# Row remainders of 64, a halved w3 product and a later weight split in the expert stage of a hybrid decoder layer

## The chip, the cores and the metric

The kernel runs on one core of a Trainium2 chip. The metric is the device time of one execution in microseconds (us), lower is better. The engines are named as in the profile: PE (TensorE matmul) and PEld (its weight loads), DVE (VectorE), ACT (ScalarE), POOL (GpSimd), SP (SyncE, here only the issuer of DMAs). PSUM is the memory that PE writes its products to.

## The reference, cut to what matters

One decoder layer over 2048 tokens of width 1024: a token mixer, then a mixture of experts, then a last norm. The change is in the experts: 32 experts of hidden width 512, each token goes to 2 of them, and each expert computes for its tokens

```
h = jax.nn.silu(xb @ w1[e]) * (xb @ w3[e])
return h @ w2[e]
```

Of the 4096 token rows the routing of the reference's inputs gives between 73 and 167 to an expert: 15 experts get at most 128, the other 17 get 129 to 167. The reference pads each expert's rows to blocks of 128.

## The kernel before, in words

The stages run one after the other: mixing branches, their merge (`merge_branches`), routing (`route`), experts (`run_experts`) and the final combination (`combine`). PE multiplies in a 32-bit format of reduced precision, so every operand is split into a high and a low part, and each product is made of three: high x high, high x low, low x high.

**Weights.** `ExpertWeights` holds w1 and w3 in four pieces of 1 MB and w2 in one piece of 2 MB, each as raw, high and low. There is one buffer of each kind. SP loads the raw pieces of the next expert, each as soon as the split of the piece before it in that buffer is done (for w2: all of `split2`). ACT writes the high part (`write_high13`, L1429; `write_high2`, L1434), and then DVE subtracts to get the low part of w1 and w3 (`write_low13`, L1438) and POOL that of w2 (`write_low2`, L1443).

**Blocks.** `over_blocks` walks over the experts and, for each, over its blocks of up to 128 rows; 49 blocks in all, one for each of the 15 small experts and two for each of the 17 others. PE does for a block, in this order: x times w1 (24 products of 512 columns, L1587), x times w3 (24 more), the transposes of the gated h (`turn_h`, L1560) and of the next block's x (`turn_x`, L1554), and then h times w2 (24 products, L1601), which waits for `split2` of the expert. ACT does tanh (L1621), copies the high parts of h (L1625) and x (L1617), and copies the result out of PSUM (L1643), each half followed by a DMA. DVE does the gate (L1664), gate times up (L1671) and the low parts (L1676, L1682). POOL gathers the rows of the block after next (L1528).

**Order around the last block of an expert.** Every engine works its queue strictly in the order written. In the last block of an expert, ACT and DVE also split the next expert's weights. Before the change ACT writes two w1 pieces right behind tanh, two w3 pieces behind the copies of h and x, then copies the result, and then writes the high part of w2; DVE splits one piece between `gate` and `gate_up` and three at the block's end. POOL splits w2 when ACT has written its high part.

**Unwritten rows.** Rows of the expert output buffer that no block writes are filled with zeros by 15 DMAs of 512 KB from SP inside the expert loop (`fill`).

Of the kernel before, what the change touches and what calls it, by code (L numbers as in the profile page):

```python
# [18 lines left out]
F32 = mybir.dt.float32  # L19
# [8 lines left out]
P = 128  # L28
# [12 lines left out]
NB = T * 2 // P + E  # L41
# [73 lines left out]
def mix_branches(nc, io, dram):  # L115
# [10 lines left out]
    with ExitStack() as ctx:  # L126
# [3 lines left out]
        def sem(name):  # L130
            return ctx.enter_context(nc.semaphore(name))
# [755 lines left out]
def merge_branches(nc, io, dram, logits):  # L887
# [14 lines left out]
    with ExitStack() as ctx:  # L902
# [23 lines left out]
        ssq, msq, rst, rh, rt = (sb(f"m_st{i}", [P, 2]) for i in range(5))  # L926

# [10 lines left out]
        half_b, dstep, passed = sem("half_bias"), sem("m_dve_step"), sem("m_passed")  # L938
        block = ctx.enter_context(nc.Block())
# [75 lines left out]
        @block.gpsimd  # L1015
        def _(pool):
            pool.memset(ident[:], 0.0).then_inc(idz, 1)
            pool.wait_ge(idz, 1)
            pool.affine_select(out=ident[:], in_=ident[:], compare_op=ALU.not_equal, fill=1.0, base=0,
                               pattern=[[-1, P]], channel_multiplier=1).then_inc(idn, 1)  # L1020

# [214 lines left out]
def route(nc, logits, table, pos, wts, ends, wt):  # L1236


    with ExitStack() as ctx:
# [3 lines left out]
        def sem(name):  # L1243
# [3 lines left out]
        NBT = table.shape[1]  # L1247
        gmax, gsum, gval = (sb(f"rt_g{i}", [P, TT]) for i in range(3))
# [5 lines left out]
        io_g, io_e, io_s, io_b, io_tok, io_blk = (sb("io_g", [P, G]), sb("io_e", [P, E]), sb("io_s", [P, P]), sb("io_b", [P, NBT]),  # L1254
                                                  sb("io_tok", [P, TT]), sb("io_blk", [P, TT]))
# [3 lines left out]
        big = sb("big", [P, E, TT])  # L1259
# [3 lines left out]
        blkf, slotf = sb("blkf", [P, TT, 2]), sb("slotf", [P, TT, 2])  # L1263
# [8 lines left out]
        def _(pool):  # L1272
# [6 lines left out]
            pool.iota(io_blk[:], [[P, TT]], base=0, channel_multiplier=0, **kw).then_inc(consts, 1)  # L1279
# [41 lines left out]
        def _(dve):  # L1321
# [29 lines left out]
            first_hot(oh[0][:], em[:], m1[:], io_e[:], E, eq[:], gi[:])  # L1351
# [3 lines left out]
            first_hot(oh[1][:], em[:], m2[:], io_e[:], E, eq[:], gi[:])  # L1355
# [16 lines left out]
            s.link(TTc(big[:], cnt[:].unsqueeze(2).to_broadcast([P, E, TT]), io_blk[:].unsqueeze(1).to_broadcast([P, E, TT]), ALU.is_gt))  # L1372
            s.link(dve.tensor_reduce(nb[:], big[:], AX.X, ALU.add))
            s.link(dve.tensor_scalar(nb[:], nb[:], 1.0, None, ALU.max))
            s.link(dve.memset(e1[:], 1.0))
            s.link(dve.tensor_tensor_scan(nbi[:], e1[:], nb[:], 0.0, ALU.mult, ALU.add))
            s.link(TTc(nbe[:], nbi[:], nb[:], ALU.subtract))
            s.mark(dve.memset(ends[:, 0:1], 0))
            s.mark(dve.tensor_copy(ends[:, 1:E + 1], nbi[:]))
            s.link(dve.tensor_scalar(nbe[:], nbe[:], float(P), None, ALU.mult))  # L1380
# [6 lines left out]
            s.mark(dve.tensor_scalar(posb[:], pos[:], 7, None, ALU.logical_shift_right))  # L1387
            s.link(dve.tensor_scalar(poss[:], pos[:], P - 1, None, ALU.bitwise_and))
            s.mark(dve.tensor_copy(blkf[:], posb[:]))
            s.link(dve.tensor_copy(slotf[:], poss[:]))  # L1390
            for k in range(2):
# [8 lines left out]
class ExpertWeights:  # L1400
# [4 lines left out]
    def __init__(self, ctx, nc, io):  # L1405
# [9 lines left out]
        self.in13, self.in2 = [sem(f"w13_in{i}") for i in range(4)], sem("w2_in")  # L1415
        self.high13, self.split13, self.high2, self.split2 = sem("w13_high"), sem("w13_split"), sem("w2_high"), sem("w2_split")
# [29 lines left out]
def run_experts(nc, dram, table, ends, wt):  # L1446
# [4 lines left out]
    with ExitStack() as ctx:  # L1451
# [7 lines left out]
        tbank, hbank, uturn, ybank = ps[0:2], ps[2:4], ps[4:6], ps[6:8]  # L1459
        xg = sb("xg", [P, D])  # L1460
        x_hi, x_lo = sb("xT_hi", [P, KD, P], F32R), sb("xT_lo", [P, KD, P], F32R)
        idx = sb("idx", [P, 1], I32)
        th, gg, hg = sb("th", [P, DE]), sb("gg", [P, DE]), sb("hg", [P, 2, HC])
        h_hi, h_lo = sb("hT_hi", [P, FE, P], F32R), sb("hT_lo", [P, FE, P], F32R)
        ysb = sb("ysb", [P, 2, 512])
        ident = sb("x_ident", [P, P])
        zeros = sb("zeros", [P, D])
        zeros_set, zeros_out = sem("zeros_set"), sem("zeros_out")
# [4 lines left out]
        y_ps, y_free, y_out = sem("y_psum"), sem("y_read"), [sem(f"y_out{i}") for i in range(2)]  # L1473
        passed = sem("x_passed")
        block = ctx.enter_context(nc.Block())

        def over_blocks(eng, block_of):
# [363 lines left out]
```

## Time and profile before

| what | value |
|---|---|
| time, median of 3 runs | 3071.8 us (3067.86 to 3072.96) |
| profiled execution: its own time | 3067.27 us |
| its span, first to last instruction | 3065.5 us |
| PE busy | 2675.9 us (87%) |
| DVE, ACT, POOL busy | 1588.1, 1021.7, 656.8 us |
| mean granted TensorE clock | 0.935 of full speed |

Times below are of the profiled execution, in us from the start of its span. A PE matmul's duration runs past the start of the next one, since matmuls are pipelined: the distance between starts is what a matmul costs.

### The profile page before, as it was taken

How to read it: one execution, taken by the hardware profiler on the slowest of the kernel's cores; microseconds unless marked ns; L12 is line 12 of the kernel's file. 1: busy time of each engine (PE TensorE's matmuls, PEld its weight loads, DVE VectorE, ACT ScalarE, POOL GpSimd, SP SyncE). 2: the span in 40 equal slices, each digit the busy share in tenths (PEclk: the TensorE clock that was granted, in tenths of full speed). 3: DMA queues.
4: the chain of work that ended last, by engine and by line, in shares of the span. 5: the costliest groups of instructions: out<-in, count | busy, mean ns of one | idle time of the engine just before them, and what ended most of it. 6: DMA issues, size and time to landing. Idle time of an engine off the chain costs nothing. (4 is left out here: it accounts for less than half of the span.)

```text
span 3065.5 us, 33795 instructions
## 1 busy us (share of the span) xinstructions
PE 2675.9 (87%) x10264; PEld 1857.8 (61%) x10265; DVE 1588.1 (52%) x2239; ACT 1021.7 (33%) x1210; POOL 656.8 (21%) x537
## 2 busy tenths in 40 slices
PE   4889898986999999999999999288999999998940
PEld 2333333434886788578858884177777777776730
DVE  8867667673444334434343344745445454455448
ACT  2121212202222222222222222155445454555531
POOL 4413132230000000000000000434334333345351
PEclk8999899987999999989998999599999999999975
DMA  5122131306334233423333333288667866679667
GB/s 161 35 83 95 41 130 41 130 21 205 99 94 152 79 99 97 144 87 94 95 140 91 99 102 132 96 313 317 233 233 265 290 240 242 229 265 345 243 257 293
DMA packets 396651, 490.97 MB, mean 160 GB/s; under 512 B 30544, under 2 KB 257104, under 8 KB 396624
## 3 DMA queue, kind: packets, MB, share of 16 engines
q1 hardware_dynamic: 370560, 421.46, 41.0%
q0 software_dynamic: 11952, 43.52, 4.0%
q10 hardware_dynamic: 14112, 25.70, 2.2%
q8 instruction: 9, 0.15, 0.0%
q14 instruction: 18, 0.15, 0.0%
HBM read 415.13 MB, written 75.50 MB: 160 GB/s over the span
## 5 line engine op out<-in xcount | busy, mean ns | idle before, releaser
L1099 PE MATMUL mrgps<-act_hi,w_hi 128*128 128x512 f32 x1280 | 503.6, 393 | 29.9 <-DVE w_lo L1167 23.5
L1099 PE MATMUL mrgps<-act_lo,w_hi 128*128 128x512 f32 x1280 | 502.2, 392 | 0.0
L1099 PE MATMUL mrgps<-act_hi,w_lo 128*128 128x512 f32 x1280 | 501.9, 392 | 0.0
L502 PE MATMUL mixps<-xT,win 128*128 128x512 f32 x896 | 410.3, 614 | 0.8 <-ACT xT L405 0.8
L1443 POOL TENSOR_TENSOR w_lo<-w_raw,w_hi 128x1024 fp32r<-128x1024 f32 x128 | 328.6, 2604 | 231.9 <-ACT w_hi L1434 231.9
L1438 DVE TENSOR_TENSOR w_lo<-w_raw,w_hi 128x2048 fp32r<-128x2048 f32 x124 | 301.0, 2468 | 36.7 <-ACT w_hi L1429 36.7
L502 PEld LDWEIGHTS mixps<-xT,win 128*128 128x128 f32 x896 | 171.6, 196 | 239.3 <-issue 235.8
L1587 PE MATMUL exps<-w_hi,xT_hi 128*128 128x512 f32 x784 | 305.8, 390 | 2.2 <-DVE xT_lo L1682 2.2
L1587 PE MATMUL exps<-w_lo,xT_hi 128*128 128x512 f32 x784 | 305.7, 390 | 0.0
L1587 PE MATMUL exps<-w_hi,xT_lo 128*128 128x512 f32 x784 | 305.6, 390 | 0.0
L1099 PEld LDWEIGHTS mrgps<-act_hi,w_hi 128*128 128x128 f32 x1280 | 243.2, 190 | 82.6 <-issue 25.0
L1099 PEld LDWEIGHTS mrgps<-act_hi,w_lo 128*128 128x128 f32 x1280 | 242.8, 190 | 51.3
L1099 PEld LDWEIGHTS mrgps<-act_lo,w_hi 128*128 128x128 f32 x1280 | 243.2, 190 | 50.3
L1274 POOL IOTA io_g<- 128x4 f32 x1 | 0.1, 145 | 1210.6 <-POOLq L902 1210.6
L1167 DVE TENSOR_TENSOR w_lo<-w_raw,w_hi 128x1280 fp32r<-128x1280 f32 x129 | 192.5, 1492 | 125.1 <-ACT w_hi L1037 123.3
L1429 ACT ACTIVATE w_hi<-w_raw 128x2048 fp32r<-128x2048 f32 x128 | 238.5, 1917 | 8.1 <-DMA w_raw<-in_expert_w_dram 8.0
L1055 ACT ACTIVATE gt<-mrgps,mb 128x512 f32<-128x512 f32 x128 | 88.2, 689 | 444.3 <-PE mrgps L1099 444.3
L1037 ACT ACTIVATE w_hi<-w_raw 128x1280 fp32r<-128x1280 f32 x129 | 164.4, 1275 | 194.9 <-DVE tmp L1189 135.3
L1119 PE MATMUL mrgps<-wout,merged 128*128 128x512 f32 x512 | 222.1, 593 | 6.7 <-DVE merged L1191 6.7
L1189 DVE SCALAR_TENSOR_TENSOR tmp<-gt,mrgps 128x512 f32<-128x512 f32 x96 | 66.0, 687 | 298.8 <-PE mrgps L1099 298.8
L1664 DVE SCALAR_TENSOR_TENSOR gg<-th,exps 128x512 f32<-128x512 f32 x49 | 33.7, 688 | 312.5 <-ACT th L1621 312.5
L1601 PE MATMUL exps<-w_hi,hT_hi 128*128 128x512 f32 x392 | 160.9, 411 | 15.2 <-POOL w_lo L1443 15.1
(334 smaller groups left out, 3588.8 us busy)
## 6 DMA issues: line engine op xcount, KB each, us to landing
w_raw<-in_expert_w_dram SPq DMA_DIRECT2D x128, 1024.0 KB, 8.7
w_raw<-in_merge_gate_w_dram SPq DMA_DIRECT2D x132, 512.0 KB, 4.1
w_raw<-in_expert_w_dram SPq DMA_DIRECT2D x32, 2048.0 KB, 9.6
win<-in_w_in_dram SPq DMA_DIRECT2D x56, 512.0 KB, 3.9
expert_rows<-ysb ACTq DMA_DIRECT2D x98, 256.0 KB, 6.1
w_raw<-in_branch_w_dram SPq DMA_DIRECT2D x132, 128.0 KB, 4.0
xin<-in_x_dram SPq DMA_DIRECT2D x20, 512.0 KB, 6.5
act_raw<-xn_feature_major SPq DMA_DIRECT2D x10, 1024.0 KB, 8.5
```

The costliest lines, as they stand in the source:

```text
L502: last = pe.matmul(ring.bank(("f", f))[:], win[:, i % NW, k], xT[:, k, :], start=(k == 0), stop=(k == KD - 1))
L1037: act.activation(w_hi[:, k % 2].rearrange("p k n -> p (k n)"), w_raw[:, k].rearrange("p k n -> p (k n)"), ACT.Copy).then_inc(w_hi_set, 1)
L1055: act.activation(gt[:], gbank[k % 2][:], ACT.Tanh, scale=0.5, bias=mb[:, k, ds(d, 1)]).then_inc(g_free, 1)
L1099: last = pe.matmul(bank[:], w[:, k % 2, kk], x[:, a], start=(kk == w_tiles[0] and x is act_hi and w is w_hi), stop=(kk == w_tiles[-1] and ...
L1119: last = pe.matmul(bbank[h][:], merged[:, kk, t * P:(t + 1) * P], wout[:, kk, h * 512:(h + 1) * 512], start=(kk == 0), stop=(kk == KD - 1))
L1167: dve.tensor_tensor(lo, w_raw[:, k].rearrange("p k n -> p (k n)"), hi.bitcast(F32), ALU.subtract).then_inc(w_split, 1)
L1189: dve.scalar_tensor_tensor(tmp[:], gt[:], 1.0, bbank[k % 2][:], ALU.add, ALU.mult).then_inc(b_free, 1)
L1429: act.activation(self.hi13[:, i], self.raw13[:, i], ACT.Copy).then_inc(self.high13, 1)
L1438: eng.tensor_tensor(self.lo13[:, i], self.raw13[:, i], self.hi13[:, i].bitcast(F32), ALU.subtract).then_inc(self.split13, 1)
L1443: eng.tensor_tensor(self.lo2[:, f], self.raw2[:, f], self.hi2[:, f].bitcast(F32), ALU.subtract).then_inc(self.split2, 1)
L1587: last = pe.matmul(hbank[w][:], x[:, k], wts_part[:, 2 * w + k // 4, cols], start=(k + n == 0), stop=(k == KD - 1 and n == 2))
L1601: last = pe.matmul(ybank[c][:], x[:, f], wts_part[:, f, c * 512:(c + 1) * 512], start=(f + n == 0), stop=(f == FE - 1 and n == 2))
```

## The change

An expert's rows past the first 128 are cut into steps of 64. Such a half block has its 64 rows twice in the 128 columns of the stationary operand, once high and once low (`BOTH`), so that two products do instead of three; the two halves of the result lie in PSUM partitions 0 to 63 and 64 to 127 and are added by DVE, after ACT has copied the upper one down. Half blocks come first, the last block of an expert is a full one. The product with w3 is made in two halves of 256 columns, in every block, so that gating can begin on the first. In the last block all four pieces of the next expert's w1 and w3 are split behind `high_h(g, 1)` on ACT and behind `low_h(g, 1)` on DVE. `turn_h(g, 1)` moves behind the first quarter (`contract(g, 0)`) of the product with w2. The zeros for the whole output buffer (8064 rows of 4 KB) are written by 32 DMAs of POOL during the merge. Routing computes the positions for the new blocks. The pieces of the diff below are, in order: PE's block, ACT's and DVE's queue in the last block of an expert (with ACT's `half_tanh` of a half block between them), POOL in the merge stage, DVE in routing.

```diff
+            def products_of(g, e4, products):
+                expand(gate_ps, 0, slice(0, DE), e4, products)
+                for j in range(2):
+                    expand(up_ps[j], 1, slice(j * HC, (j + 1) * HC), e4, products)
+                turn_h(g, 0)
+                turn_x(g + 1, 0)
+                turn_x(g + 1, 1)
+                pe.wait_ge(wt.split2, e4 + 4)
+                contract(g, 0, products)
+                turn_h(g, 1)
+                for f in range(1, FE):
+                    contract(g, f, products)
+
+            def block_products(parts, k, hi, lo):
+                return (parts[:, k, HIGH], hi), (parts[:, k, LOW], hi), (parts[:, k, HIGH], lo)
+
+            def half_products(parts, k, hi, lo):
+                return (parts[:, k, BOTH], hi), (parts[:, k, BOTH], lo)
...
                 final = pe.snap(b1 - 1)
+                with pe.If(b0 < final):
+                    with pe.Fori(b0, final) as g:
+                        half_block(g, e4)
+                one(final, e4)
...
                 tanh(g)
-                if nxt is not None:
-
-                    for i in range(2):
-                        wt.write_high13(act, nxt, i)
-                high_h(g, 0)
-                high_x(g + 1)
-                high_h(g, 1)
-                if nxt is not None:
-                    for i in range(2, 4):
+                high_h(g, 0, P)
+                high_x(g + 1, 0)
+                high_x(g + 1, 1)
+                high_h(g, 1, P)
+                if nxt is not None:
+                    for i in range(4):
                         wt.write_high13(act, nxt, i)
                 for n in range(2):
                     act.wait_ge(y_ps, g * 2 + (n + 2))
...
                 if nxt is not None:
                     wt.write_high2(act, nxt)
...
+            def half_tanh(g):
+                act.wait_ge(h_ps, g * 3 + 3)
+                act.activation(hrow[:, 0], gate_ps[HB:P, :], ACT.Copy).then_inc(high_set, 1)
+                act.wait_ge(sum_set, g * 3 + 1)
+                act.activation(th[0:HB], gate_ps[0:HB, :], ACT.Tanh, scale=0.5).then_inc(tanh_d, 1)
...
                 gate(g)
-                if nxt is not None:
-                    wt.write_low13(dve, nxt, 0)
-                gate_up(g)
-                low_h(g, 0)
-                low_x(g + 1)
-                low_h(g, 1)
-                if nxt is not None:
-                    for i in range(1, 4):
+                gate_up(g, 0)
+                gate_up(g, 1)
+                dve.sem_inc(sum_set, 3)
+                low_h(g, 0, P)
+                low_x(g + 1, 0)
+                low_x(g + 1, 1)
+                low_h(g, 1, P)
+                if nxt is not None:
+                    for i in range(4):
                         wt.write_low13(dve, nxt, i)
...
+            with pool.Fori(0, TRIPS * KD) as i:
+                pool.wait_ge(w_split, i * SU + 1)
+                pool.dma_start(dram["y"][ds(i * FILL, FILL), :].rearrange("(p r) (q n) -> p (r q) n", r=2, n=256),
+                               zeros[:].unsqueeze(1).to_broadcast([FILL // 2, 2 * D // 256, 256])).then_inc(zeros_out, 16)
...
-            s.link(TTc(big[:], cnt[:].unsqueeze(2).to_broadcast([P, E, TT]), io_blk[:].unsqueeze(1).to_broadcast([P, E, TT]), ALU.is_gt))
+            s.link(TTc(big[:], cnt[:].unsqueeze(2).to_broadcast([P, E, NSTEP]), io_over[:].unsqueeze(1).to_broadcast([P, E, NSTEP]), ALU.is_gt))
...
+            s.link(dve.tensor_scalar(backf[:], backf[:], -1.0, 0.0, ALU.add, ALU.max))
+            s.link(dve.scalar_tensor_tensor(backm[:], backf[:], 1.0, backf[:], ALU.min, ALU.add))
+            s.link(TTc(blkf[:], blkf[:], backf[:], ALU.subtract))
+            s.link(dve.scalar_tensor_tensor(slotf[:], backm[:], -float(HB), slotf[:], ALU.mult, ALU.add))
+            s.link(TTc(ei[:], ei[:], blkf[:], ALU.add))
+            s.link(dve.scalar_tensor_tensor(posf[:], ei[:], float(HB), slotf[:], ALU.mult, ALU.add))
```

The semaphores of the mixing stage are now given back at the start of the merge stage. `NB`, the bound on the number of blocks and the width of the routing table, grows from 64 to 94, and `NSTEP` is 30 where the routing compared against 16 thresholds.

## Rows read from the trace of the kernel before

**Rows 1.** The page, busy time of PE.
```profile
PE 2675.9 (87%) x10264; PEld 1857.8 (61%) x10265; DVE 1588.1 (52%) x2239; ACT 1021.7 (33%) x1210; POOL 656.8 (21%) x537
```

**Rows 2.** Stretches: length, busy PE, PEld, DVE, ACT, POOL, clock, DMA share, GB/s.
```profile
890.00:1968.00 1078.00, 1010.32 (x4076) 754.19 (x4074) 450.65 (x679) 284.77 (x302) 29.21 (x16) 0.95 0.35 109
2045.00:3010.00 965.00, 849.06 (x3907) 687.69 (x3905) 473.50 (x509) 493.69 (x574) 388.10 (x245) 0.97 0.74 267
```

**Rows 3.** Timeline of PE: the first expert product and the last block's w2 product.
```profile
1994.65 0.79 PE L1587 MATMUL exps<-w_hi,xT_hi 128*128 128x512 f32 x1 [2.18 <-DVE xT_lo L1682]
...
2948.10 0.47 PE L1601 MATMUL exps<-w_hi,hT_hi 128*128 128x512 f32 x1 [0.80 <-POOL w_lo L1443]
```

**Rows 4.** Timeline of a block whose expert has two; start, length, engine, line.
```profile
2300.34 0.50 PE L1601 MATMUL exps<-w_hi,hT_hi 128*128 128x512 f32 x1
...
2301.29 0.39 ACT L1625 ACTIVATE hT_hi<-exps 128x256 fp32r<-128x256 f32 x1
...
2301.56 3.73 ACT L1429 ACTIVATE w_hi<-w_raw 128x2048 fp32r<-128x2048 f32 x2
...
2302.49 6.68 DVE L1438 TENSOR_TENSOR w_lo<-w_raw,w_hi 128x2048 fp32r<-128x2048 f32 x3
...
2305.62 0.60 ACT L1643 ACTIVATE ysb<-exps 128x512 f32<-128x512 f32 x1 [0.33 <-PE exps L1601]
...
2306.04 0.39 PE L1587 MATMUL exps<-w_hi,xT_hi 128*128 128x512 f32 x1
...
2307.97 3.90 ACT L1434 ACTIVATE w_hi<-w_raw 128x1024 fp32r<-128x1024 f32 x4 [0.54 <-ACT ysb L1643]
...
2309.11 9.42 POOL L1443 TENSOR_TENSOR w_lo<-w_raw,w_hi 128x1024 fp32r<-128x1024 f32 x4 [6.62 <-ACT w_hi L1434]
...
2316.70 0.39 PE L1587 MATMUL exps<-w_hi,xT_lo 128*128 128x512 f32 x1
2317.60 0.44 PE L1560 MATMUL exps<-x_ident,hg 128*128 128x128 f32 x2 [0.51 <-DVE hg L1671]
2317.88 1.04 PE L1554 MATMUL exps<-x_ident,xg 128*128 128x128 f32 x8
2318.07 0.38 ACT L1625 ACTIVATE hT_hi<-exps 128x256 fp32r<-128x256 f32 x1 [5.72 <-PE exps L1560]
...
2318.97 0.50 PE L1601 MATMUL exps<-w_hi,hT_hi 128*128 128x512 f32 x1
```

**Rows 5.** Timeline of a block that is the only one of its expert.
```profile
2744.86 0.37 SPq L1424 DMA_DIRECT2D w_raw<-in_expert_w_dram  x1
2745.07 0.47 PE L1601 MATMUL exps<-w_hi,hT_hi 128*128 128x512 f32 x1 [0.55 <-POOL w_lo L1443]
...
2753.83 3.90 ACT L1434 ACTIVATE w_hi<-w_raw 128x1024 fp32r<-128x1024 f32 x4 [1.68 <-DMA w_raw<-in_expert_w_dram]
2754.97 11.50 POOL L1443 TENSOR_TENSOR w_lo<-w_raw,w_hi 128x1024 fp32r<-128x1024 f32 x4 [8.19 <-ACT w_hi L1434]
...
2760.23 4.01 DVE L1438 TENSOR_TENSOR w_lo<-w_raw,w_hi 128x2048 fp32r<-128x2048 f32 x1 [1.30 <-ACT w_hi L1429]
...
2764.63 0.44 PE L1560 MATMUL exps<-x_ident,hg 128*128 128x128 f32 x2 [2.82 <-DVE hg L1671]
...
2766.71 0.76 PE L1601 MATMUL exps<-w_hi,hT_hi 128*128 128x512 f32 x1
...
2773.42 0.39 PE L1587 MATMUL exps<-w_hi,xT_hi 128*128 128x512 f32 x1
```

**Rows 6.** Stretch behind that block's stall, columns as in rows 2.
```profile
2766.71:2769.70 2.99, 2.99 (x9) 2.37 (x10) 2.86 (x4) 2.99 (x5) 0.98 (x1) 0.62 0.68 212
```

**Rows 7.** Groups by line and shape, routing; count, busy us, mean ns, idle before.
```profile
L1317 PE MATMUL rtps<-U,V 128*128 128x66 f32 x32 | 7.2, 403 | 31.1 <-DVEq L1395 31.1
...
L1393 DVE TENSOR_TENSOR U<-io_b,blkf 128x1056 fp32r<-128x1056 f32 x2 | 2.5, 1252 | 0.0
...
L1372 DVE TENSOR_TENSOR big<-rt_c,io_blk 128x512 f32<-128x512 f32 x1 | 0.7, 691 | 0.0
```

More of the change, by code:

```diff
@@ L40 @@
 R = G + E
-NB = T * 2 // P + E
+HB = P // 2
+PARTS = 5
+BOTH, HIGH, LOW = slice(0, P), slice(HB, HB + P), slice(HB + P, HB + 2 * P)
+NSTEP = (T - P) // HB
+NB = 94
 EPS = 1e-6
@@ L1485, in expert @@
                     with eng.Fori(b0, last) as g:
-                        block_of(g, None)
-                block_of(last, eng.snap(e + 1) if split else None)
+                        half_block(g, e)
+                block_of(last, e, split)
             with eng.Fori(0, E - 1) as e:
@@ L1549, in _, with turn_x @@
         def _(pe):
-            def turn_x(g):
-                pe.wait_ge(gathered, g * 16 + 16)
-                for h in range(2):
-                    for k in range(4):
-                        last = pe.transpose(tbank[h][:, k * P:(k + 1) * P], xg[:, (4 * h + k) * P:(4 * h + k + 1) * P], ident[:])
+            def turn_x(g, h):
+                if h == 0:
+                    pe.wait_ge(gathered, g * 16 + 16)
+                for k in range(4):
+                    last = pe.transpose(tbank[h][:, k * P:(k + 1) * P], xg[:, (4 * h + k) * P:(4 * h + k + 1) * P], ident[:])
@@ L1565, in _, with expand @@
-            pe.sem_inc(h_ps, 1)
+            def expand(bank, w, cols, e4, products):
+                for k in range(KD):
+                    if k % 4 == 0:
+                        pe.wait_ge(wt.split13, e4 + (2 * w + k // 4 + 1))
+                    part = slice(k % 4 * DE + cols.start, k % 4 * DE + cols.stop)
+                    for n, (x, weights) in enumerate(products(xT, k, wt.hi13, wt.lo13)):
+                        last = pe.matmul(bank[:, 0:cols.stop - cols.start], x, weights[:, 2 * w + k // 4, part],
+                                         start=(k + n == 0), stop=(k == KD - 1 and weights is wt.last13))
+                last.then_inc(h_ps, 1)
@@ new lines, in contract @@
+            def contract(g, f, products):
+                if f % 2 == 0:
+                    pe.wait_ge(h_split, g * 2 + (f // 2 + 2))
+                for c in range(2):
+                    if f == 0:
+                        pe.wait_ge(y_free, g * 2 + (c + 2))
+                    for n, (x, weights) in enumerate(products(hT, f, wt.hi2, wt.lo2)):
+                        last = pe.matmul(ybank[c][:], x, weights[:, f, c * 512:(c + 1) * 512],
+                                         start=(f + n == 0), stop=(f == FE - 1 and weights is wt.last2))
+                    if f == FE - 1:
+                        last.then_inc(y_ps, 1)
@@ L1638, in one @@
+            def one(g, e, split):
+                nxt = act.snap(e + 1) if split else None
+                tanh(g)
+                act.sem_inc(high_set, 3)
+                act.sem_inc(y_high_set, 2)
+                high_h(g, 0, P)
+                high_x(g + 1, 0)
+                high_x(g + 1, 1)
+                high_h(g, 1, P)
+                if nxt is not None:
+                    for i in range(4):
                         wt.write_high13(act, nxt, i)
@@ new lines, in half_block @@
+            def half_block(g, e):
+                half_gate(g)
+                half_gate_up(g, 0)
+                half_gate_up(g, 1)
+                low_h(g, 0, HB)
+                low_x(g + 1, 0)
+                low_x(g + 1, 1)
+                low_h(g, 1, HB)
+                for n in range(2):
+                    dve.wait_ge(y_high_set, g * 2 + (n + 1))
+                    dve.wait_ge(y_out[n], g * 16 + 16)
+                    dve.scalar_tensor_tensor(ysb[0:HB, n], ybank[n][0:HB, :], 0.5, yrow[:, n], ALU.mult, ALU.add).then_inc(y_free, 1)
@@ L1697, in _ @@
-            over_blocks(dve, one)
+            low_x(0, 0)
+            low_x(0, 1)
+            over_blocks(dve, half_block, one)
 def combine(nc, io, dram, pos, wts, out):
```

232 lines of the change are left out of this document (125 added, 107 removed).

## The prediction

> **What bounds the kernel now.** I read the page first: PE is busy for 87% of the span, so the first question is whether PE sets the pace where the change works [rows 1]. The stretches say where that is: the merge stage runs PE at 1010 of 1078 us, the expert loop at 849 of 965 us, and there the other engines and the DMAs are much busier than anywhere else (DMA share 0.74 against 0.35) [rows 2]. The expert loop lasts from the first product with w1 at 1994.65 to the last block's w2 product at 2948.10, 953.5 us [rows 3]. I mark a block by S, the start of its product with w2, and ask what lies between two S.
>
> In an expert with two blocks S is at 2300.34 and next at 2318.97, 18.63 us [rows 4]. PE's own work there is 24 products with w2 in 5.70 (2300.34 to 2306.04), 48 with w1 and w3 in 10.88 (the last starts 10.66 after the first, so 0.227 each), and 2.05 for gate and transposes. So PE sets it. But a second chain ends at almost the same time: result copy on ACT (2305.62), high part of w2 (2307.97), POOL's four subtractions (2309.11, 9.42 long, to 2318.53). It has 0.4 us to spare. The product with w2 waits for all four.
>
> In an expert with one block S is at 2745.07 and next at 2766.71, 21.64 us [rows 5]. There it is the single w2 buffer: SP can load it only when the split before is done (2744.86), ACT waits for the DMA until 2753.83, POOL starts at 2754.97 and needs 11.50. Meanwhile PE waited 2.82 for DVE, whose w1 piece of 4.01 stood between the gate and its product.
>
> **What the change takes away.** A second block has at most 39 rows more than 128 (the largest expert has 167), so all 17 second blocks become half blocks. Each saves a third of its 72 products: 24 x 0.23 = 5.5 us of PE, 94 us in all. The gate no longer stands behind the end of w3: the tail from the first transpose to S is 2317.60 to 2318.97, 1.37 us, and the 0.9 ahead of it goes [rows 4]. The 2.82 of rows 5 goes too.
>
> **What it adds to the second chain.** Every expert now runs through this chain once, from the S of its predecessor's last block to its own first S, whether its first block is full or half, since `products_of` waits for `split2` in both:
> - six products with w2 before `turn_h(g, 1)`, 2300.34 to about 1.5 later (a quarter of 5.70 is 1.43): 1.50
> - transposes to the copy of h, 2317.60 to 2318.07: 0.47; copy to first w1 copy, 2301.29 to 2301.56: 0.27
> - four w1 and w3 pieces on ACT, two take 3.73: 7.35. Until now two stood here, and they hid under the products with w2, whose end released the result copy at 5.28. Now ACT gets to it 9.6 after S
> - two result copies with their DMA issues, 2305.62 to 2307.97: 2.35; to POOL's start, 1.14
> - POOL's four subtractions: 9.42 uncontended [rows 4], 11.50 where DVE splits a piece meanwhile [rows 5]
> - POOL's end (2766.47) to S (2766.71): 0.24 [rows 5]
>
> Sum 22.7 us with 9.42. I take that value, because DVE's four pieces are ready early: the first starts 1.9 behind ACT's first (POOL's wait behind its own ACT pass is 1.14 for a pass of half the size), each is 2.23 (a third of 6.68), so the last ends about 10.9 after ACT's first piece, when POOL is just starting. With 11.50 the chain would be 24.8.
>
> The Trainium skill, "SBUF — State Buffer", section "Who interferes with whom", says that a VectorE instruction with two SBUF inputs and a GpSimd instruction that reads SBUF block each other; the two durations above agree. By that rule nothing of DVE's gating (one SBUF input, one in PSUM) would delay POOL, and the sum stays at 22.7.
>
> PE's own way from S to the next S is shorter: w1 can start at 6.5 (first piece low at 2.2 + 1.9 + 2.3), then 5.44 + 5.8 + 1.4, 19.1 for a full block. So PE waits about 3.5 us behind the transposes in full first blocks, and some 7 in half ones. After the stall of 2.82 and the transposes, nine products started in 2.99 us and the granted clock was 0.62, the lower level of 1.2 GHz for a part [rows 6]; the 24 products took 6.71 instead of 5.70 (2766.71 to 2773.42) [rows 5]. I take 1.1 us for each S behind such a wait: above 1.01, as these waits are longer. Lower bound nothing.
>
> The Trainium skill, "TensorE: Matmul & The Clock Gate", Part 4, "PE-mode transpose", says that transposes do not release the clock as other work does. The trace shows a fall right behind eight of them; by the rule the transposes between the waits would not save the clock, which favours the 1.1.
>
> This 1.1 also delays `turn_h(g, 1)`: chains that begin at a cold S are 23.8. These are the 13 one-block experts after the first; 18 chains (17 behind two-block experts, one behind the first expert) are 22.7.
>
> **Inside a two-block expert**, from the half block's S to the full block's S: 16 products with w2 and two transposes 3.8 + 0.2, cold 1.1, w1 5.44, w3 in 48 products of 256 columns, tail 1.37. The trace has no 256-column product. Lower bound: half of 0.227, 0.113. Upper bound: the weight load's 0.19 would be laid bare; but pairs of load and 128-column transpose start every 0.11 (eight in 1.04) [rows 4], so a load needs no more than that. Near that row I take 0.120: 5.8 us. Sum 17.7. Half-block gating on ACT and DVE (a copy, an add, tanh, two multiplies and adds more) begins when ACT has done its w2 pass, 15.8 after S, and takes some 5.3 us by the durations of such rows: ready at 21.1, hidden under the chain by 1.6. If POOL were faster than that, this would be the next late thing.
>
> **Sum, expert loop.** Start to first S 5.44 + 5.8 + 1.4 + 1.1 = 13.7; 18 x 22.7 = 408.6; 13 x 23.8 = 309.4; 17 x 17.7 = 300.9. Total 1032.6 against 953.5: +79. Last product cold: +1.
>
> **The rest.** Routing on DVE: compare and reduce over 960 instead of 512 elements, 0.69 to about 1.27 each, +1.2; four passes over the table's width 96 for 66, 1.25 to 1.8: 4 x 0.57 = +2.3 [rows 7]; about seven small operations more at 0.2, +1.4; the 16 last table products took 0.22 each at 66 columns (half of 7.2 us), bounds nothing and 1.6, taken +0.8. Together +6. Zeros: 33 MB in the merge stage, where the DMA share is 0.35 and POOL has 29 of 1078 us of work [rows 2]; weights are loaded four units ahead. Taken +1, bounds nothing and, if each of the 32 DMAs held up PE by 1 us, +32. The 15 zero DMAs leave the expert loop, where no w2 wait depends on them any more: nothing. SP's four loads are issued later, behind each split, and w2's behind POOL, as before; its about 9 us end before ACT's 12, so the old bound of the one-block experts is covered. If that cover went, loads would be the next late thing. Freeing semaphores in another place: nothing, perhaps 1.
>
> Total +87: 3067.3 + 87 = 3154 for the profiled execution. The median of before lies 4.5 above its profiled one, so 3159.
>
> **Rivals.**
> - *The chain binds, but the clock does not fall* (0.18). For it: one-block waits are only 0.7 longer than the 2.82 that cost the clock, and the transposes now come before the wait. Against: rows 6. It takes back 32 x 1.1 = 35: 3124.
> - *Faster: the chain stays where it was and PE's saving comes through* (0.03). If ACT's four pieces hid under the w2 products as two do now, a chain would be 18.4, as in rows 4: 31 x 18.4 + 17 x 16.6 + 13 = 866, -88 + 7, about 2991. It decides at a mean chain of 20.4 us (953.5 - 13.7 - 300.9 - 8, by 31). Against: the w2 products last 5.7 and four copies need 7.35 behind 2.2; nothing in ACT's order lets the result copy pass.
> - *256-column products are bound by their weight loads at 0.19* (0.07): 17 x 48 x 0.07 = +57, 3216. Only the full blocks behind half ones pay; the others have it under the chain.
> - *DVE and POOL still collide* (0.05), at 11.50: 31 x 2.1 = +65, 3224. For it: they miss each other by almost nothing.
> - *The zeros hold up the merge* (0.05), about +32: 3191.
>
> **How the numbers follow.** The likeliest case, chain with a fallen clock, has 0.60: 3159, its own range 3140 to 3178 (0.113 for 0.120 is -6, routing and zeros a few us either way, the 1.1 between 1.0 and 1.3). No measurable change has 0.02. A measurement of this kernel tells 0.2%, 6 us, from nothing. All cases but the faster one and that of no change lie above it: slower 0.95, same 0.02, faster 0.03. The range reaches down to the case of the unfallen clock with its own spread, 3112, and up to the zeros, 3192; left out are the faster case, the bare weight loads and the collision, 0.17 together.
>
> **What the profile after would show.** POOL's subtractions near 2.36 us each instead of 2.60; ACT's result copy in last blocks held up by w1 and w3 copies and no longer by PE; about 22.7 to 23.8 from the last S of an expert to the next expert's first S, and PE idle before the w2 product with POOL as releaser, in nearly all 31; 17 to 18 us from a half block's S to the full one's; PE's busy time down, the span up; clock in the expert loop under 0.97. I am wrong if POOL's end comes before PE's tail in most experts, or if the time between these marks is not what grew.

## The result and the profile after

| what | before | after |
|---|---|---|
| time, median | 3069.9 us (3067.86 to 3072.96, 4 runs) | 3162.7 us (3158.86 to 3164.76, 4 runs) |
| ratio | | 1.030, 95% interval 1.0284 to 1.0315 |
| profiled execution, its span | 3067.27, 3065.5 us | 3164.76, 3163.2 us |
| granted clock, whole span | 0.935 | 0.911 |

The forecast was 3159 us, slower. I first divide the 97.7 us by which the span grew, at the same marks as in the prediction. The last run of 16 logit products of the merge starts at 1922.73 against 1915.77 (+7.0); from there to the first product with w1, 2009.68, the routing and the first gather take 8.1 us more; the expert loop from that product to the last S takes 1034.2 against 953.5 (+80.7); after the last S there are 119.3 us against 117.4 (+1.9).

The page, busy times of the engines:

```profile
PE 2675.6 (85%) x10896; PEld 1882.3 (60%) x10897; DVE 1652.5 (52%) x2433; ACT 1041.8 (33%) x1261; POOL 657.2 (21%) x569
```

Against [rows 1] PE is busy for the same 2676 us. The change took products away, but a product at the lower clock counts for nearly twice as long. The busy total alone would say that nothing was saved. The two stretches of [rows 2], now:

```profile
core 0: us, PE busy (x) PEld busy (x) DVE busy (x) ACT busy (x) POOL busy (x), PEclk, DMA share, GB/s
890.00:1968.00 1078.00, 1017.23 (x4105) 759.99 (x4103) 446.77 (x661) 287.04 (x304) 53.23 (x42) 0.96 0.42 134
2045.00:3010.00 965.00, 829.63 (x4366) 693.81 (x4367) 492.79 (x609) 496.75 (x598) 316.00 (x205) 0.92 0.66 231
```

In the expert loop PE is less busy in the same stretch, and the clock is down to 0.92. One chain from the S of an expert's last block to the next expert's first S, in the timeline. A row is start, duration, engine, line and operation, and in brackets the idle time before and what ended it:

```profile
2339.06 0.70 PE L1595 MATMUL exps<-w_hi,hT_parts 128*128 128x512 f32 x2
...
2340.53 0.38 PE L1575 MATMUL exps<-x_ident,hg 128*128 128x128 f32 x2
...
2340.95 0.39 ACT L1672 ACTIVATE hT_parts<-exps 128x256 fp32r<-128x256 f32 x1 [1.30 <-PE exps L1575]
...
2341.23 7.31 ACT L1456 ACTIVATE w_hi<-w_raw 128x2048 fp32r<-128x2048 f32 x4
...
2343.16 8.89 DVE L1465 TENSOR_TENSOR w_lo<-w_raw,w_hi 128x2048 fp32r<-128x2048 f32 x4 [1.38 <-ACT w_hi L1456]
...
2345.51 0.50 PE L1584 MATMUL exps<-w_hi,xT_parts 128*128 128x512 f32 x1 [0.41 <-DVE w_lo L1465]
...
2348.43 0.59 ACT L1706 ACTIVATE ysb<-exps 128x512 f32<-128x512 f32 x1
...
2350.82 3.90 ACT L1461 ACTIVATE w_hi<-w_raw 128x1024 fp32r<-128x1024 f32 x4 [0.55 <-ACT ysb L1706]
2351.96 9.35 POOL L1470 TENSOR_TENSOR w_lo<-w_raw,w_hi 128x1024 fp32r<-128x1024 f32 x4 [10.80 <-ACT w_hi L1461]
...
2358.32 0.44 PE L1575 MATMUL exps<-x_ident,hg 128*128 128x128 f32 x2 [3.08 <-DVE hg L1750]
```

and where it ends, with the products with w2 of the half block behind it:

```profile
2361.36 0.79 PE L1595 MATMUL exps<-w_hi,hT_parts 128*128 128x512 f32 x1 [1.20 <-POOL w_lo L1470]
2361.95 0.63 PE L1595 MATMUL exps<-w_lo,hT_parts 128*128 128x512 f32 x1
2362.38 0.63 PE L1595 MATMUL exps<-w_hi,hT_parts 128*128 128x512 f32 x1
...
2365.36 0.59 PE L1595 MATMUL exps<-w_hi,hT_parts 128*128 128x512 f32 x1
2365.79 0.41 PE L1595 MATMUL exps<-w_lo,hT_parts 128*128 128x512 f32 x1
2366.03 0.39 PE L1595 MATMUL exps<-w_hi,hT_parts 128*128 128x512 f32 x1
```

Read the first fence from start to start along the chain: S, transposes, h's copy, four w1 and w3 copies, the result copy, w2's high part, POOL, and in the second fence the next S, 22.30 us later. ACT's result copy comes 9.37 us behind S; nothing but ACT's own w1 and w3 copies stands ahead of it (its row has no idle time before it), where in [rows 4] it came 5.28 behind S. In the second fence the starts lie 0.43 us apart at first and 0.24 later. The clock of that stretch, and of the same work behind an S without a wait:

```profile
2361.36:2365.40 4.04, 4.04 (x11) 3.16 (x12) 0.85 (x2) 0.28 (x1) 1.05 (x2) 0.50 0.75 258
2339.06:2345.10 6.04, 6.04 (x26) 4.57 (x26) 4.31 (x6) 4.74 (x6) 1.15 (x2) 1.00 0.29 87
```

PEclk is 0.50, the 1.2 GHz level, for the first 4 us behind this S, where PE had waited 3.08 and 1.20 us. Behind the S at 2339.06, whose row shows no wait, it is 1.00. The groups of the loop by line:

```profile
line engine op names shapes xcount | busy us, mean ns | idle before us <-releasers
...
L1470 POOL TENSOR_TENSOR w_lo<-w_raw,w_hi 128x1024 fp32r<-128x1024 f32 x124 | 290.7, 2378 | 349.1 <-ACT w_hi L1461 349.1
L1465 DVE TENSOR_TENSOR w_lo<-w_raw,w_hi 128x2048 fp32r<-128x2048 f32 x124 | 275.8, 2286 | 42.7 <-ACT w_hi L1456 42.7
...
L1595 PE MATMUL exps<-w_hi,hT_parts 128*128 128x512 f32 x636 | 254.6, 466 | 64.1 <-POOL w_lo L1470 62.2
...
L1575 PE MATMUL exps<-x_ident,hg 128*128 128x128 f32 x194 | 46.4, 328 | 52.1 <-DVE hg L1750 52.1
```

POOL's subtraction takes 2.38 us in the mean, as in the chain of [rows 4] that nothing disturbed (9.42 for four). PE waits 62.2 us for POOL ahead of w2 (31 times) and 52.1 for the half blocks' gating (17 times, 3.1 each). The rows of the routing that answer to [rows 7]:

```profile
L1335 PE MATMUL rtps<-U,V 128*128 128x96 f32 x32 | 7.3, 413 | 35.4 <-DVEq L1421 35.4
...
L1419 DVE TENSOR_TENSOR U<-io_b,blkf 128x1536 fp32r<-128x1536 f32 x2 | 3.5, 1750 | 0.0
```

### The profile page after: what moved, and what is told of

Read it like the earlier page. It is cut to its first block and busy times, and to the rows that moved or that the text cites. A ratio compares the mean times of both kernels' runs of the same rounds, so it can differ in the third digit from the quotient of the medians.

```text
span 3163.2 us, 35670 instructions
## 1 busy us (share of the span) xinstructions
PE 2675.6 (85%) x10896; PEld 1882.3 (60%) x10897; DVE 1652.5 (52%) x2433; ACT 1041.8 (33%) x1261; POOL 657.2 (21%) x569
## 5 line engine op out<-in xcount | busy, mean ns | idle before, releaser
L1584 PE MATMUL exps<-w_hi,xT_parts 128*128 128x256 f32 (+1 forms) x1944 | 472.6, 323 | 29.7 <-DVE w_lo L1465 25.3
L1584 PEld LDWEIGHTS exps<-w_hi,xT_parts 128*128 128x128 f32 x1944 | 335.2, 191 | 84.1 <-DVE w_lo L1465 54.4
L1470 POOL TENSOR_TENSOR w_lo<-w_raw,w_hi 128x1024 fp32r<-128x1024 f32 x128 | 300.0, 2377 | 349.1 <-ACT w_hi L1461 349.1
L1584 PE MATMUL exps<-w_lo,xT_parts 128*128 128x256 f32 (+1 forms) x1176 | 365.2, 319 | 0.0
L1595 PE MATMUL exps<-w_hi,hT_parts 128*128 128x512 f32 x648 | 259.4, 466 | 64.1 <-POOL w_lo L1470 62.2
L1465 DVE TENSOR_TENSOR w_lo<-w_raw,w_hi 128x2048 fp32r<-128x2048 f32 x124 | 275.8, 2286 | 42.7 <-ACT w_hi L1456 42.7
L1034 POOL DMA_DIRECT2D expert_rows<-zeros x32 | 29.8, 932 | 1078.2 <-DVE w_lo L1183 1024.7
L1584 PEld LDWEIGHTS exps<-w_lo,xT_parts 128*128 128x128 f32 x1176 | 224.1, 191 | 15.1
```

The lines of the kernel that those rows point to most:

```text
L1465: eng.tensor_tensor(self.lo13[:, i], self.raw13[:, i], self.hi13[:, i].bitcast(F32), ALU.subtract).then_inc(self.split13, 1)
L1470: eng.tensor_tensor(self.lo2[:, f], self.raw2[:, f], self.hi2[:, f].bitcast(F32), ALU.subtract).then_inc(self.split2, 1)
L1584: last = pe.matmul(bank[:, 0:cols.stop - cols.start], x, weights[:, 2 * w + k // 4, part], start=(k + n == 0), stop=(k == KD - 1 and weigh ...
L1595: last = pe.matmul(ybank[c][:], x, weights[:, f, c * 512:(c + 1) * 512], start=(f + n == 0), stop=(f == FE - 1 and weights is wt.last2))
```

## The experiments

Each trace was read at the same marks. "Chain" is from the S of an expert's last block to the next expert's first S, in the mean of 31; "half to full" from a half block's S to its full block's S, in the mean of 17; "loop" from the first product with w1 to the last S. In before the 17 are second blocks of 128. All in us. A ratio below is to runs of the kernel before taken beside that experiment, whose medians lay between 3068.6 and 3072.8. "Undone, filled" and the like name versions described further down.

```
kernel                      median   loop     chain   half to full
before                      3069.9    953.5   20.08   18.62
after                       3162.7   1034.2   22.70   18.58
ACT's order undone          3116.1    987.8   21.11   18.70
ACT's and DVE's undone      3078.8    955.4   20.00   18.81
POOL leaves one pass out    3077.5    951.4   20.58   17.52
fill in all blocks          3167.3   1039.1   22.38   19.24
fill in first blocks        3118.3    995.9   22.42   16.64
zeros twice                 3167.3   1035.5   22.72   18.57
w2's last pass on DVE       3149.6   1020.0   22.86   17.39
undone, last pass on DVE    3084.5    958.7   20.75   17.64
undone, filled              3049.8    920.4   20.03   16.65
before, filled              3073.4    956.4   20.07   18.63
```

**Undo ACT's order.**

```diff
 tanh(g)
+if nxt is not None:
+    for i in range(2):
+        wt.write_high13(act, nxt, i)
...
 high_h(g, 1, P)
-    for i in range(4):
+    for i in range(2, 4):
         wt.write_high13(act, nxt, i)
```

> Edit: ACT copies the first two w1 pieces of the next expert right behind tanh again, two stay behind the last copy of h; DVE's order is left as in the changed kernel. Theory 1 (the chain from one last S to the next expert's first S sets the pace, and ACT's four copies ahead of the result copy are what made it longer): the result copy starts about 6 us after S instead of 9.4, the chain falls from 22.3 to about 19 to 20 (POOL and DVE will overlap for a pass or so), the waits behind it get shorter and some clock is kept: 31 x 2.5 + 14, about 90 us less than the changed kernel, near 3070. Rival (the half blocks' extra work on ACT and DVE, or the products of 256 columns, made it slower): within 10 us of the changed kernel, 3155 to 3165.

Measured: 3116.1 us (3111.44 to 3117.2, 4 runs), ratio 1.0157 (1.014 to 1.0174). Half of what the theory promised. The timeline of one chain:

```profile
2487.03 0.71 PE L1595 MATMUL exps<-w_hi,hT_parts 128*128 128x512 f32 x2
...
2489.68 8.89 DVE L1465 TENSOR_TENSOR w_lo<-w_raw,w_hi 128x2048 fp32r<-128x2048 f32 x4
...
2496.36 11.41 POOL L1470 TENSOR_TENSOR w_lo<-w_raw,w_hi 128x1024 fp32r<-128x1024 f32 x4 [7.22 <-ACT w_hi L1461]
...
2507.82 0.79 PE L1595 MATMUL exps<-w_hi,hT_parts 128*128 128x512 f32 x1 [3.80 <-POOL w_lo L1470]
```

POOL starts 9.3 us behind S instead of 12.9, as the theory has it. But DVE's fourth piece still runs until 2498.57, and POOL's four passes then take 11.41 instead of 9.35. DVE's late pieces, harmless in the changed kernel, cost 2 us per chain as soon as POOL is early.

**Undo both orders.** As above, and on DVE the first piece between `gate` and `gate_up`:

```diff
 gate(g)
+if nxt is not None:
+    wt.write_low13(dve, nxt, 0)
 gate_up(g, 0)
...
-    for i in range(4):
+    for i in range(1, 4):
         wt.write_low13(dve, nxt, i)
```

> Edit: both orders of before in the last block, ACT's as in the run with ACT's alone and DVE's first piece between the gate and its product again. Theory 1: DVE's first piece now coincides with POOL's passes, which then take about 11.5 in place of 9.4, so a part of the gain is given back: about 60 to 80 us less than the changed kernel, 3080 to 3100. Rival (only the pair of orders matters, DVE's lateness is what PE waits for): clearly faster than ACT's order alone, below 3060. Rival (extra work is to blame): within 10 us of the changed kernel.

Measured: 3078.8 us (3076.11 to 3081.42, 5 runs), ratio 1.0035 (1.0021 to 1.0049). The order of the split is worth 84 of the 93 us (79 of the loop's 81). I had expected it to end above the run with ACT's order alone; it ends below. With one DVE piece gone early, the other three are done when POOL starts, so the chains into half blocks have no collision: ten of the 17 take 18.7 us. In the 14 chains into a full block (21.1 in the mean) DVE's early piece meets one of POOL's passes 13 times, as forecast. What is left above the kernel before, 9 us, is spent ahead of the experts: the first product with w1 is at 2004.38 here, 9.7 later than in before. So the half blocks and the halved w3 products, under the old order, gain nothing in the loop (955.4 against 953.5); the filled version of this order, below, shows what took the gain back.

**POOL's passes.** POOL leaves out the last of the four subtractions of w2 from the second expert on, so the low part of that quarter stays that of the first expert.

```diff
+if f == 3 and skip:
+    eng.sem_inc(self.split2, 1)
+    continue
 eng.tensor_tensor(self.lo2[:, f], ...)
...
-wt.write_low2(pool, pool.snap(e + 1))
+wt.write_low2(pool, pool.snap(e + 1), True)
```

> Edit: POOL leaves out the last of its four subtractions for w2 of every expert but the first (the low part of the last quarter of w2 keeps its first content; that part of the result is not the reference's). Theory 1: the chain is 2.36 us shorter. In front of a full first block PE has 3.4 us to give, so it gains all of it, 14 x 2.36 = 33; in front of a half block PE's gating is ready only 1.2 before POOL, so 17 x 1.2 = 20. About 53 us less than the changed kernel, near 3110. Rival (POOL is not on the path that sets the end): no change.

Measured: 3077.5 us (3066.75 to 3086.82, 10 runs), ratio 1.0029 (1.0014 to 1.0044). The chain follows POOL, 22.70 to 20.58, and "half to full" fell as well, 18.58 to 17.52, where nothing was taken away. The second effect was the clock: with shorter waits fewer products run at the lower level, and a half block's products with w2 take 4.95 us from S to the next product with w1 instead of 6.01, which is all of the 1.06. The forecast of this run had left that out, and 3077.5 is 33 below it.

**Keep TensorE busy in its waits.** Products of 256 columns, whose result is overwritten, stand in PE's queue ahead of and behind the transposes: 22 and 8 in half blocks, 24 in full ones.

```diff
+fill(g, 22)   # half blocks only
 turn_h(g, 0)
 turn_x(g + 1, 0)
 turn_x(g + 1, 1)
+fill(g, 8 if half else 24)
 pe.wait_ge(wt.split2, e4 + 4)
```

> Edit: PE fills its waits ahead of the product with w2 with products of 256 columns whose result nobody reads: 24 in a full block, 22 and 8 in a half block (ahead of and behind the transposes). They take less time than the waits last. Theory 1 with the clock as a price of its own: the fall of the clock costs about 0.8 us in each of 13 chains and 2.1 in each of 17 half blocks, so filled waits give back about 46 us, near 3117, with chains of 22.3 everywhere and 16.6 from a half block's S to the full one's. Rival (the slow first products after a wait come from something else, such as queue start-up): no change.

Measured: 3167.3 us (3165.64 to 3169.67, 4 runs), ratio 1.033 (1.0313 to 1.0347). This was a badly made test. The fill also stood in the full block behind a half block, where PE waits for nothing: from that block's first product to its S it now took 15.17 us instead of 12.57, 17 times 2.6. In the half blocks the effect was there: 4.08 us in the mean from S to the next product with w1, instead of 6.01.

**The same, only where PE waits.** In full blocks the 24 stand only if the block is its expert's first; the half blocks keep their 22 and 8.

```diff
-fill(g, 24)
+with pe.If(g < b0 + 1):
+    fill(g, 24)
```

> The changed kernel, with TensorE filling its waits by 256-column products whose result nobody uses, this time only in the first block of each expert, which is where it waits: 24 of them behind the transposes of a block of 128 that is its expert's only one, 22 and 8 in a block of 64. Theory (in its waits TensorE loses its full clock, and that costs 2.0 us in each of 17 blocks of 64 and 0.7 to 0.8 in each of 13 chains that end in a block of 128; the full block behind a block of 64, which got 2.6 us of fill for nothing in the run before this one, has none now): 3162.7 - 17 x 2.0 - 13 x 0.75 = 3119 us, with 4.0 us from the half block's start with w2 to its next product in place of 6.05, and 12.6 in place of 15.2 in the full block behind it. Rival (the slow products cost nothing on the chain, or filling costs as much as it saves in any place): 3155 to 3170 us.

Measured: 3118.3 us (3115.41 to 3121.75, 4 runs), ratio 1.016 (1.0137 to 1.0183). PE's timeline, one half block and its successor:

```profile
2298.81 2.80 PE L1603 MATMUL exps<-w_hi 128*128 128x256 f32 x22
2302.04 0.44 PE L1575 MATMUL exps<-x_ident,hg 128*128 128x128 f32 x2 [0.43 <-DVE hg L1763]
2303.10 1.19 PE L1603 MATMUL exps<-w_hi 128*128 128x256 f32 x8
2305.18 0.50 PE L1595 MATMUL exps<-w_hi,hT_parts 128*128 128x512 f32 x1 [0.89 <-POOL w_lo L1470]
```

The next product with w1 is at 2309.27, 4.09 behind S, and the granted clock from 2045 to 2900 is 1.00 instead of 0.91. "Half to full" fell by 1.94, the chain by 0.28. In the loop that is 17 x 1.94 + 31 x 0.28 = 41.7, less 3.2 for fill in the very first block: 38.5, and 38.3 measured. The median fell by 44, some of it scatter ahead of the loop (its first product is at 2002.25 here). So about 40 of the 93 us were the clock: PE does more work and no weight is ready earlier, and yet the kernel is faster.

**Twice the zeros.** Behind each zero DMA a second one of the same size to a spare tensor.

```diff
+pool.dma_start(dram["spare"][ds(i * FILL, FILL), :]..., zeros...).then_inc(zeros_out, 16)
```

> The changed kernel, with every DMA of zeros in the merge stage followed by a second one of the same 1008 KB to a spare tensor in DRAM: twice the zero traffic, nothing else. Theory A (the 6.7 us by which the merge grew come from the zeros' share of the DMA engines): the last logit product comes another 6 to 8 us later, and with it the time, 3169 to 3171 us. Theory B (the transfers are hidden and the 6.7 us come from something else that the change moved): no change, within 2 us.

Measured: 3167.3 us (3164.91 to 3170.04, 4 runs), ratio 1.0321 (1.0299 to 1.0343). The median is 4.6 above the changed kernel's. The intervals of the two ratios overlap, though all four runs lie above the changed kernel's four, the lowest by 0.15 us. The profiled execution has its first product with w1 at 2008.38, 1.3 earlier than the changed kernel's. With one set of zeros that mark lay between 2002.25 and 2014.19 in nine traces (mean 2007.1); before's, in two, at 1994.65 and 1996.04. Of the 11.7 between the means 8.1 are routing and first gather (8.1 to 8.4 in every trace); the 3.6 left in the merge are smaller than the scatter. What the zeros cost stays open, between nothing and some 5 us. Neither theory is shown.

**w2's last pass on DVE.** All work is done.

```diff
 # POOL
-wt.write_low2(pool, pool.snap(e + 1))
+wt.write_low2(pool, pool.snap(e + 1), range(3))
 # DVE, behind its four w1 and w3 pieces
+wt.write_low2(dve, nxt, range(3, 4))
```

> The changed kernel, with the last of the four w2 subtractions moved from GpSimd to VectorE, behind its four w1 and w3 pieces; all work is done. Theory (the chain from one product with w2 to the next is set by GpSimd's fourth subtraction of 2.38 us; VectorE is idle from about 13 us behind the start, and its own pass takes some 1.2): almost the time of the run in which that subtraction was left out, 3077.5 us, plus 0.5 us of later gating in each of 17 blocks of 64, so 3080 to 3092 us. Rival (VectorE's part in the gating becomes the chain, or its pass and GpSimd's collide as in the run with ScalarE's order of before): above 3120 us.

Measured: 3149.6 us (3140.24 to 3155.05, 4 runs), ratio 1.025 (1.0224 to 1.0276). The theory was wrong, the rival right in both its parts:

```profile
2192.04 8.01 POOL L1470 TENSOR_TENSOR w_lo<-w_raw,w_hi 128x1024 fp32r<-128x1024 f32 x3 [10.79 <-ACT w_hi L1461]
...
2194.83 0.59 ACT L1662 ACTIVATE h_high_rows<-exps 64x512 f32<-64x512 f32 x1
2194.84 3.01 DVE L1470 TENSOR_TENSOR w_lo<-w_raw,w_hi 128x1024 fp32r<-128x1024 f32 x1 [2.69 <-ACT w_hi L1461]
...
2196.72 3.33 POOL L1470 TENSOR_TENSOR w_lo<-w_raw,w_hi 128x1024 fp32r<-128x1024 f32 x1
...
2197.78 0.68 DVE L1739 TENSOR_TENSOR exps<-exps,h_high_rows 64x512 f32<-64x512 f32 x1
...
2200.71 0.69 PE L1575 MATMUL exps<-x_ident,hg 128*128 128x128 f32 x2 [5.36 <-DVE hg L1750]
```

(The row at 2196.72 is the third of POOL's three passes by itself.) DVE's pass takes 3.01 us beside POOL's, and POOL's three take 8.01 instead of 7.1. The times fit two passes that take turns: POOL's second pass runs until 2196.77, 1.93 behind the start of DVE's; DVE's ends 1.08 later, about half of the 2.29 that it needs for a piece of twice the size; and POOL's third ends 2.21 behind that. DVE's pass also stands ahead of the half block's gating (2197.78, where the changed kernel had it 0.63 behind ACT's copy), and PE waits 5.36 for it. Chains into half blocks rise to 24.0 us, those of single blocks fall to 21.5. The old order with the same pass on DVE:

> The version with ScalarE's and VectorE's order of before (two w1 pieces behind tanh, one subtraction behind the gate; 3078.8 us) and with the last of the four w2 subtractions moved from GpSimd to VectorE behind its pieces; all work is done. Theory (GpSimd is still the end of the chain in blocks of 64, by 1.8 us, and by about 1 in the rest, and the wait costs clock besides): 17 x 1.3 to 2.0 + 13 x 0.5 to 1.5 less, 3030 to 3055 us, below the kernel before. Rival (at 18.75 us the chain is already bound by the products and the gating, and no more is to be had there): 3070 to 3080 us.

Measured: 3084.5 us (3079.57 to 3088.88, 6 runs), ratio 1.0048 (1.003 to 1.0066), against 3078.8 without. The same two effects: DVE's pass takes 3.06 us in the mean, and chains into half blocks rise from 19.1 to 20.2. Neither forecast held.

**The old order, filled.** To the version with both orders undone, fill of 16 and 12 in half blocks and of 18 in single ones.

> The version with ScalarE's and VectorE's order of before (3078.8 us) and TensorE's waits in the first block of each expert filled by 256-column products whose result nobody uses: 16 ahead of the transposes of the gated rows and 12 behind all transposes in a block of 64, 18 ahead of them in a block of 128 that is its expert's only one. Theory (at the 18.75 us chain of the old order the lost clock costs as much as at 22.3: 6.3 us from a half block's start with w2 to the next product, where 4.1 is the time at full clock, 17 times, and 0.5 to 1.5 behind a block of 128 that stands alone, 13 times): 3078.8 - 17 x 2.2 - 13 x 0.7 = 3032 us, 3025 to 3045, which is under the kernel before. Rival (the fill comes in the way of the products, since the waits are only some 2 us each here): 3065 to 3090 us.

Measured: 3049.8 us (3042.93 to 3050.67, 6 runs), ratio 0.9924 (0.991 to 0.9938): faster than both kernels. The gain of 29 us is below the 47 expected. "Half to full" fell by 2.16, 17 times, 37 us, as forecast; the chain did not move (20.00 to 20.03), so the 9 us of the single blocks did not come, and the first product with w1 happened to lie 5.9 later. The loop alone fell by 34.9, to 920.4, which is 33 below that of the kernel before. This is what the half blocks and halved w3 products gain once the clock is kept; in the version with both orders undone the clock took it back.

**The kernel before, filled.** 20 products ahead of the transposes in experts with one block.

```diff
+with pe.If(b1 < b0 + 2):
+    for _ in range(20):
+        pe.matmul(ybank[0][:, 0:256], ...)
 turn_h(g, 0)
```

> The kernel before, with 20 products of 256 columns whose result nobody uses ahead of the transposes of the gated rows in each expert that has one block only, where TensorE waits 2.8 to 4.2 us. Theory (what the clock costs behind a wait is not the changed kernel's own): the stretch from a start with w2 to the next product, 6.1 to 6.9 us behind such a wait against 5.7 elsewhere, comes down to 5.7, and the first product with w2 stands 0.3 us earlier: 0.6 to 1.5 us in each of 13 experts, 3050 to 3062 us. Rival (no effect, as the wait is on the chain and the slow products are not): 3066 to 3073 us.

Measured: 3073.4 us (3068.7 to 3080.58, 12 runs), ratio 1.001 (0.9999 to 1.002). The rival was right in its cause, and its range ended 0.4 lower. PE's rows of one expert and the next:

```profile
2109.98 2.55 PE L1593 MATMUL exps<-w_hi 128*128 128x256 f32 x20
2113.87 0.44 PE L1560 MATMUL exps<-x_ident,hg 128*128 128x128 f32 x2 [1.34 <-DVE hg L1675]
2115.94 0.47 PE L1605 MATMUL exps<-w_hi,hT_hi 128*128 128x512 f32 x1 [0.54 <-POOL w_lo L1443]
2121.61 0.39 PE L1587 MATMUL exps<-w_hi,xT_hi 128*128 128x512 f32 x1
2133.17 0.44 PE L1560 MATMUL exps<-x_ident,hg 128*128 128x128 f32 x2 [0.52 <-DVE hg L1675]
2136.70 0.47 PE L1605 MATMUL exps<-w_hi,hT_hi 128*128 128x512 f32 x1 [2.00 <-POOL w_lo L1443]
```

The same place in the kernel before, unfilled:

```profile
2112.68 0.78 PE L1601 MATMUL exps<-w_hi,hT_hi 128*128 128x512 f32 x1
2118.79 0.39 PE L1587 MATMUL exps<-w_hi,xT_hi 128*128 128x512 f32 x1
2130.37 0.44 PE L1560 MATMUL exps<-x_ident,hg 128*128 128x128 f32 x2 [0.51 <-DVE hg L1671]
2132.63 0.47 PE L1601 MATMUL exps<-w_hi,hT_hi 128*128 128x512 f32 x1 [0.73 <-POOL w_lo L1443]
```

The products behind S are done in 5.67 us instead of 6.11, and the next wait for POOL is 2.00 instead of 0.73. Time saved ahead of a wait that another chain ends is given back in the wait.

## Why the prediction was right

**What bounds the kernel now.** Confirmed: at 18.6 us per block PE's work and the chain of splits end together in before, and whatever lengthens the chain shows at once. The order of the split alone, ACT's and DVE's, moves 79 of the loop's 81 us.

**The chain.** Its steps, forecast and measured in the chain shown: 1.50 and 1.47, 0.47 and 0.42, 0.27 and 0.28, 7.35 and 7.20, 2.35 and 2.39, 1.14 and 1.14, 9.42 and 9.35, 0.24 and 0.05. Sum 22.7 and 22.30. The 20 that begin at full clock take 22.34 in the mean. Behind an S whose products ran at the lower clock there were 11 and not 13; they take 22.6 to 23.9, 23.3 in the mean, forecast 23.8. The 31 chains took 703.6 us, forecast 718.0: 14.4 too much.

**Uncontended POOL.** The choice of 9.42 over 11.50 was right (mean 2378 ns a pass), and by as little as said: DVE's last piece ends at 2352.05, POOL starts at 2351.96. The undone ACT order shows the other case at 11.41. The Trainium skill, "SBUF — State Buffer", section "Who interferes with whom", has such instructions block each other, and gating from PSUM not. The traces agree in both. POOL's four take 9.35 with the half block's gating beside them. The run with w2's last pass on DVE shows the block: its 3.01 us are 1.93 of waiting for POOL's pass and 1.08 of its own, where half of a piece's 2.29 would be 1.15, and POOL's next pass then takes 3.33 instead of 2.38. In [rows 5] the same accounts for DVE's 4.01, of which 1.86 is waiting, and for POOL's 11.50, whose fourth pass takes 4.42 there.

**Clock.** The lower level came in the waits as forecast, but it was mis-sized: 1.1 us for each S behind a wait, taken from one row of 1.01 with a wait of 2.82. In half blocks it cost 1.9 to 2.0 (6.01 in the mean, against 3.8 + 0.2 forecast for the work, and 4.08 in the filled version), since 4 us of products ran at 0.50. That makes "half to full" 18.58 instead of 17.7, 15 us in all, and it cancels the overestimated chain. The loop came out at 1034.2 against 1032.6 by this cancellation. That closeness is luck: two errors of 15 us with opposite signs. By stages the span grew by 7.0, 8.1, 80.7 and 1.9 (merge, routing and gather, loop, end) for 1, 6, 79 and 1 forecast, 10.7 more in all. That the median is only 4 off comes besides from the 4.5 added for its distance to the profiled execution; after, the median lies 2 below it. The fill experiment gives the clock's whole share: about 40 us, where the rival of an unfallen clock had 35. It is not a part beside the order's 84: under the old order the same fill gives the loop 35 back as well, so most of this loss comes with the half blocks and not with the new order.

**Half blocks.** 256-column products: 0.120 taken; in the block shown the second of 24 such products starts at 2352.34 and the 24th at 2354.97, which gives 0.1195. The gating was forecast ready 21.1 behind S; its first part was in use at 19.3 and its second ready at 20.1, hidden under POOL's chain by about 1.2 us (PE's wait for POOL ahead of S). The run with a pass on DVE shows it as the next late thing, as the prediction named it.

**The rest.** Routing: widening cost 0.50 a pass over the table (forecast 0.57), the table's products 0.01 each. The routing's own work came to +4.4, forecast +6. What the forecast missed is the first gather: PE waited 10.9 us for it instead of 6.9, 10.85 to 11.18 in every trace with the new routing, and I had nothing for that. Routing and gather together are +8.1 for a forecast of +6. The traces point to a cause. In before, first fence, POOL issues the gather 3.10 us ahead of SP's first weight loads; in the changed kernel, second fence, the loads go 1.23 ahead of it.

```profile
1985.82 1.16 POOL L1528 DMA_INDIRECT xg<-xn,idx  x1 [0.96 <-POOL idx L1525]
...
1988.92 3.28 SPq L1421 DMA_DIRECT2D w_raw<-in_expert_w_dram  x4
```

```profile
1996.08 2.65 SPq L1448 DMA_DIRECT2D w_raw<-in_expert_w_dram  x4
...
1997.31 1.07 POOL L1541 DMA_INDIRECT xg<-xn,idx  x1 [1.05 <-issue]
...
2005.84 1.94 PE L1569 MATMUL exps<-x_ident,xg 128*128 128x128 f32 x8 [10.88 <-DMA xg<-xn,idx]
```

In before SP waited for `zeros_set`, a memset that stands behind the gather in POOL's queue. That wait went with the zeros, which the prediction had at nothing for the expert loop, and the gather now takes 8.4 us from issue to landing instead of 4.6. The order is the same in all ten traces of the new kernel's versions and in both of the old one's; no run put the wait back, so the cause is argued and not shown.

Zeros, forecast +1: in the pair of traces the merge ended 7.0 later, but the same mark scatters by 12 us between traces of the new kernel's versions, and what the zeros cost is not told apart from that. PE's busy time did not go down as I said, but stayed, for the clock.

## What to carry to other kernels

Before moving work behind a hand-over, follow the chain that this work delays, not the share of the engine that does it: ACT was busy for a third of the time, and its order alone decided 47 us, with DVE's 84. A wait that is taken away can matter too: it may have kept a large transfer behind a small one that is waited for. If TensorE waits some microseconds and then has a short piece of work on the critical chain, the lower clock nearly doubles the time of its products (0.43 us each for 0.24), and useless products in the wait can pay for themselves (44 us here); but only where the wait is, and only if the work behind it is what sets the next step. Work moved from a late engine to an idle one must be priced beside what runs at that moment, and with what it stands ahead of.

## What the runs showed of the hardware that was not expected

The time at the lower level was longer behind the half blocks' waits than behind that of [rows 6]: about 4 us at a granted clock of 0.50 after waits of 3.1 and 1.2 us with ten transposes between them; 24 to 30 products of fill in each expert's first block kept it at 1.00 from 2045 to 2900 us, although 0.4 and 0.9 us of wait and the transposes were left. A DVE subtraction of 1024 columns that started during one of POOL's of the same form took 3.03 us in the mean of 31, in the one shown 1.93 until POOL's pass ended and 1.08 for itself; so a short pass on an idle DVE cost more time than POOL's own 2.38. The first gather took 8.4 us from issue to landing with four weight loads issued 1.2 us ahead of it, and 4.6 with them issued 3.1 behind it.
